# A hybrid encoder block: another order of the products, segment sums from running sums, and masked dt on ScalarE

## The reference

```
h = RMSNorm(x);  proj = h @ W_in        # columns: z | xBC | dt_f | dt_b | q | k | v | gate_a | gate_b
A: xBC = silu(centred depthwise conv of 5 taps);  xs, B, C = xBC   # 32 heads of 64, 8 groups, state 128
   per direction (forward, backward): dt = softplus(dt_raw + bias);  a = -exp(a_log) * dt
     chunks of 128 tokens, per head:
     decay[l,s] = exp(cumsum(a)[l] - cumsum(a)[s])   for s <= l, else 0
     y = (C B^T * decay * dt) @ xs  +  C @ state_in * exp(cumsum(a));  states pass between chunks
   y = y_f + y_b + d_skip * xs;  y = groupwise RMSNorm(y * silu(z)) * g;   branch_a = y @ W_ssm_up
B: q, k normed per head and rotated, softmax over all 256 tokens;  branch_b = y_attn @ W_attn_up
x = x + (sigmoid(gate_a) * branch_a + sigmoid(gate_b) * branch_b) @ W_out
x = x + relu(RMSNorm(x) @ W1)^2 @ W2;   out = RMSNorm(x)
```

## Time and profile before

| | |
|---|---|
| median of 3 runs | 1761.25 us |
| the profiled execution: its time | 1762.39 us |
| its span | 1760.6 us |
| mean granted TensorE clock | 0.981 of full speed |
| TensorE / ScalarE / VectorE / GpSimd busy | 1691.5 / 789.3 / 1071.3 / 210.3 us |
| DMA | 301.52 MB, mean 171 GB/s |

### The profile page before, as it was taken

The page is one execution under the profiler, slowest core; times in us unless marked ns, Lnnn a source line. Parts: engine busy times, 40 slices in busy tenths (PEclk is TensorE's granted clock), DMA queues, the critical chain, the costliest instruction groups (busy, mean ns, idle before and its releaser), DMA issues.

```text
span 1760.6 us, 21838 instructions
## 1 busy us (share of the span) xinstructions
PE 1691.5 (96%) x7734; PEld 1401.5 (80%) x7734; DVE 1071.3 (61%) x1190; ACT 789.3 (45%) x996; POOL 210.3 (12%) x178
## 2 busy tenths in 40 slices
PE   6888888899999999999999999999999999999997
PEld 5677677788888888888888888888888888888886
DVE  4989999966678855454545554455445544554453
ACT  4343333455455544444443445533553355335543
POOL 0445554400132200000000000000000000000000
PEclk8999989999999999999999999999999999999999
DMA  7344344456654456565655566566656665666663
GB/s 220 108 126 118 96 113 119 127 177 183 188 157 135 143 179 187 194 183 196 183 195 186 179 204 187 184 194 193 186 182 195 194 177 186 196 194 180 185 201 121
DMA packets 197222, 301.52 MB, mean 171 GB/s; under 512 B 14368, under 2 KB 70288, under 8 KB 197008
## 3 DMA queue, kind: packets, MB, share of 16 engines
q1 hardware_dynamic: 196960, 300.27, 56.4%
q10 hardware_dynamic: 176, 0.07, 0.0%
HBM read 298.20 MB, written 2.10 MB: 171 GB/s over the span
## 4 chain that ended last, share of the span: by engine, by line
issue 68%; PE 19%; DVE 9%; SPq 1%; DMA 1%; POOL 1%; ACT 0%; DVEq 0%; ACTq 0%; POOLq 0%
PE G L1216 5%; PE G L1217 5%; PE G L1218 5%; DVE acc L826 3%; DVE wlo L686 2%; PE S L1337 1%; DVE mw L876 1%; DVE acc L822 1%; DMA raw<-in_w_in 1%; DVE prob L973 0%; PE S L1224 0%; POOL q_rs L1097 0%; SPq L384 0%; PE S L1346 0%; DVE pT_lo L978 0%
## 5 line engine op out<-in xcount | busy, mean ns | idle before, releaser
L686 DVE TENSOR_TENSOR wlo<-raw,whi 128x1024 fp32r<-128x1024 f32 x560 | 698.7, 1253 | 514.3 <-ACT whi L425 514.2
L425 ACT ACTIVATE whi<-raw 128x1024 fp32r<-128x1024 f32 x560 | 593.8, 1060 | 883.8 <-PE G L1218 848.4
L1216 PE MATMUL G<-whi,a_hi 128*128 128x512 f32 x1344 | 538.2, 400 | 9.0 <-DVE wlo L686 9.0
L1217 PE MATMUL G<-wlo,a_hi 128*128 128x512 f32 x1344 | 529.8, 394 | 0.0
L1218 PE MATMUL G<-whi,a_lo 128*128 128x512 f32 x1344 | 529.2, 394 | 0.0
L1216 PEld LDWEIGHTS G<-whi,a_hi 128*128 128x128 f32 x1344 | 256.8, 191 | 61.7 <-DVE wlo L686 8.6
L1218 PEld LDWEIGHTS G<-whi,a_lo 128*128 128x128 f32 x1344 | 256.1, 191 | 55.4
L1217 PEld LDWEIGHTS G<-wlo,a_hi 128*128 128x128 f32 x1344 | 256.6, 191 | 51.1
L1216 PE MATMUL G<-whi,b_hi 128*128 128x512 f32 x640 | 250.5, 391 | 1.5 <-issue 1.5
L1218 PE MATMUL G<-whi,b_lo 128*128 128x512 f32 x640 | 249.2, 389 | 0.0
L1217 PE MATMUL G<-wlo,b_hi 128*128 128x512 f32 x640 | 249.0, 389 | 0.0
(11 more groups left out here) (188 smaller groups left out, 1347.2 us busy)
## 6 DMA issues: line engine op xcount, KB each, us to landing
raw<-in_w_in SPq DMA_DIRECT2D x136, 512.0 KB, 4.0
raw<-in_w_mlp_in SPq DMA_DIRECT2D x128, 512.0 KB, 3.8
raw<-in_w_mlp_out SPq DMA_DIRECT2D x128, 512.0 KB, 4.4
raw<-in_w_in SPq DMA_DIRECT2D x72, 256.0 KB, 2.8
raw<-in_w_in SPq DMA_DIRECT2D x144, 128.0 KB, 3.2
raw<-in_w_ssm_up SPq DMA_DIRECT2D x32, 512.0 KB, 4.4
raw<-in_w_attn_up SPq DMA_DIRECT2D x32, 512.0 KB, 4.5
raw<-in_w_out SPq DMA_DIRECT2D x32, 512.0 KB, 4.5
```

Source lines behind the costliest of these rows:

```text
L425: act.activation(whi[:, slot, 0:width], raw[:, slot, 0:width], ACT.Copy).then_inc(hi_made, 1)
L686: dve.tensor_tensor(wlo[:, slot, 0:width], raw[:, slot, 0:width], whi[:, slot, 0:width].bitcast(F32), ALU.subtract).then_inc(lo_made, 1)
L1216: pe.matmul(out_ap, hi[:, k, cols], w_hi, start=start, stop=False)
L1217: pe.matmul(out_ap, hi[:, k, cols], w_lo, start=False, stop=False)
```

## The change

1. **Order of the products.** The gates' eight products move from the merge into the scan stage: xbc 0, gate 0, xbc 1, gate 1 and so on. `conv(i)` is beside gate i, `scan(i-1)` and the gate's tanh beside xbc i. The tanh of all gates stays in a new tile `gates` of 8 blocks, whose first half is the place of `x_sb`; x is read again from HBM when the `out` products begin. The merge has only ssm_up and attn_up products, and its result goes to `a_hi`/`a_lo`.
2. **Segment sums.** Once, four small matmuls make the running sums of a for all 64 rows (32 heads, two directions), and `cum` and `neg_cum` hold them (high part in the first 64 partitions, low part in the others). Per group, `pick` selects rows: for each half (two heads) and direction TensorE does four matmuls of 256 columns, cum[l] - cum[s], into two banks; the smaller of the two directions is taken by VectorE after ScalarE has copied one (`f_made`, `seg_made`), then Exp.
3. **Masked dt** is 16 ScalarE copies of 128x128 with a scale operand per group; VectorE adds the two directions. GpSimd keeps `t2` only.
4. **The head.** The parameter DMAs are spread between pieces 5, 6, 7 and the next product's fifth; the dt product moves from piece 3 to piece 5; the dt chain's Exp and the steps behind it come later; the rope tables go to `tables` in window (1, 1).
5. The loop over the xbc windows runs 6 times over two windows (before: 2 times over two); the loop over the gates' windows is gone.

```diff
 def walk(eng, window):
     window(0, 0, "xbc", 0, [("rates", 0)])
-    window(0, 1, "xbc", 1, [("conv", 0), ("decays", 0)])
-    window(1, 0, "xbc", 2, [("conv", 1), ("scan", 0)])
-    window(1, 1, "xbc", 3, [("conv", 2), ("scan", 1)])
-    with eng.Fori(1, 3) as i:
-        window(i + 1, 0, "xbc", 2 * i + 2, [("conv", 2 * i + 1), ("scan", 2 * i)])
-        window(i + 1, 1, "xbc", 2 * i + 3, [("conv", 2 * i + 2), ("scan", 2 * i + 1)])
-    window(4, 0, "z", 0, [("conv", 7), ("scan", 6)])
...
+    window(0, 1, "gate", 0, [("conv", 0), ("decays", 0)])
+    window(1, 0, "xbc", 1, [("scan", 0), ("gate", 0)])
+    window(1, 1, "gate", 1, [("conv", 1), ("tables", 0)])
+    with eng.Fori(2, GROUPS) as i:
+        window(i, 0, "xbc", i, [("scan", i - 1), ("gate", i - 1)])
+        window(i, 1, "gate", i, [("conv", i)])
+    window(8, 0, "z", 0, [("scan", 7), ("gate", 7)])
...
-    with eng.Fori(0, 3) as j:
-        window(2 * j + 10, 0, "ssm_up", j, [("gate_b", j)])
...
+    window(13, 0, "ssm_up", 0, [("attend", 2), ("rope", 4)])
+    window(13, 1, "ssm_up", 1, [("attend", 3), ("gated_a", 0)])
...
+    window(15, 1, "attn_up", 1, [("merged", 0)])
...
@@ sync: window
-                if isinstance(r, int) and (r, par, p) == (0, 0, RING):
-                    parameters()
+                if isinstance(r, int) and (r, par, p) == (0, 0, 5):
+                    row_parameters()
+                if isinstance(r, int) and (r, par, p) == (0, 0, 6):
+                    rate_parameters(0, dt_bias_f, a_log_f)
+                    rate_parameters(1, dt_bias_b, a_log_b)
+                if isinstance(r, int) and (r, par, p) == (0, 0, 7):
+                    scan_parameters()
+                if isinstance(r, int) and (r, par, p) == (0, 1, 4):
+                    rope_parameters()
+                if kind == "out" and (idx, p) in ((0, 0), (1, 0)):
+                    sp.wait_ge(merge_v, 3 + idx)
+                    for c in range(3 * idx, 3 + idx):
+                        sp.dma_start(x_sb[:, c, :, :], x_k[:, :, c * N:(c + 1) * N]).then_inc(s_x[c], 16)
@@ scalar: decays
+            if p == 0:
+                act.wait_ge(dt_v, 4)
+                act.activation(u_dt[:, 2, :], u_dt[:, 1, :], ACT.Exp).then_inc(dt_e, 1)
...
+        def masked_dt(g, heads):
+            for h in heads:
+                for c in range(TB):
+                    for d in range(2):
+                        rate = dtv[:, c, d, ds(g * 4 + h, 1)]
+                        last = act.activation(mw[:, d, h, c, :], masks[:, 2 + d, :], ACT.Copy, scale=rate)
+            last.then_inc(mw_made, 1)
@@ scalar: conv
+            if p == 3:
...
+                act.activation(pick[:, :, :, :], sel[:, :, ds(g * 4, 4)].unsqueeze(3).to_broadcast([P, 2, 4, P]),
+                               ACT.Copy).then_inc(pick_made, 1)
+                masked_dt(g, (0,))
+            if p == 4:
+                masked_dt(g, (1, 2))
+            if p == 5:
+                masked_dt(g, (3,))
@@ scalar: scan
+            if p in (2, 4):
+                half = p // 2 - 1
+                act.wait_ge(fb_mm, 2 * g + (half + 1))
+                act.activation(ex[:, 2 * half:2 * half + 2, :].rearrange("p h l -> p (h l)"), S[:, 0, :], ACT.Copy
+                               ).then_inc(f_made, 1)
+            if p in (3, 5):
+                half = p // 2 - 1
+                act.wait_ge(seg_made, 2 * g + (half + 1))
+                part = ex[:, 2 * half:2 * half + 2, :].rearrange("p h l -> p (h l)")
+                act.activation(part, part, ACT.Exp).then_inc(ex_made, 1)
@@ vector: scan
+            if p == 0:
+                dve.wait_ge(mw_made, 3 * g + 3)
+                dve.tensor_tensor(w, w, mw[:, 1, :, :, :].rearrange("p h c l -> p h (c l)"), ALU.add
+                                  ).then_inc(scan_v, 1)
+            if p == 1:
+                dve.wait_ge(score_mm, g + 1)
...
+            if p in (2, 4):
+                half = p // 2 - 1
+                dve.wait_ge(f_made, 2 * g + (half + 1))
+                part = ex[:, 2 * half:2 * half + 2, :].rearrange("p h l -> p (h l)")
+                dve.tensor_tensor(part, part, S[:, 1, :], ALU.min).then_inc(seg_made, 1)
+            if p == 5:
+                dve.wait_ge(scan_v, step(2))
+                dve.wait_ge(ex_made, 2 * g + 2)
+                dve.tensor_tensor(w, w, ex[:, :, :], ALU.mult).then_inc(scan_v, 1)
@@ tensor: decays
+                for c in range(TB):
+                    for d in range(2):
+                        last = pe.matmul(S[:, 2, c * P:(c + 1) * P],
+                                         avx[:, c, d, :, :, :].rearrange("p a b h -> p (a b h)"), masks[:, 2 + d, :],
+                                         start=(d == 0), stop=(d == 1))
@@ tensor: scan
+            if p in (1, 3):
+                half = p // 2
+                if half:
+                    pe.wait_ge(seg_made, 2 * g + 1)
...
+                for d in range(2):
+                    for h in range(2):
+                        pe.matmul(S[:, d, h * T:(h + 1) * T], pick[:, d, 2 * half + h, :], cum[:, :],
+                                  start=(h == 0), stop=False)
+                    both = S[:, d, :].rearrange("p (h c l) -> p h c l", h=2, c=TB)
+                    for c in range(TB):
+                        last = pe.matmul(both[:, :, c, :], neg_cum[:, c * P:(c + 1) * P],
+                                         pick[:, d, 2 * half:2 * half + 2, :], start=False, stop=(c == TB - 1))
+                last.then_inc(fb_mm, 1)
...
+            if p == 6:
+                pe.wait_ge(scan_v, g * SCAN_V + 4)
+                for c in range(TB):
+                    for h in range(4):
...
+                last.then_inc(y_mm, 1)
```

More of the change, by code:

```diff
@@ L98, in walk @@
+    window(15, 0, "attn_up", 0, [("gated_a", 3)])
+    window(15, 1, "attn_up", 1, [("merged", 0)])
+    window(16, 0, "attn_up", 2, [("merged", 1)])
+    window(16, 1, "attn_up", 3, [("merged", 2)])
     window(17, 0, "out", 0, [("merged", 3)])
@@ L119, in piece_number, with landed_count @@
     return r * (2 * PIECES) + (PIECES * par + p)
[L122 to L128, removed]
+def landed_count(r, par, p, early):
+    if p >= PIECES:
+        r, par, p = (r + 1, 0, p - PIECES) if par else (r, 1, p - PIECES)
+    use = p // RING + 1
+    if early or (isinstance(r, int) and r <= GROUPS):
+        return r * 128 + (96 + 16 * use if par else 48 * use)
+    return r * 64 + (par * 32 + use * 16 + 64 * (GROUPS + 1))
 def previous(r, par):
@@ L172, in build @@
     raw = place("raw", [P, RING, 2 * N])
-    x_sb = place("x_sb", [P, TB, D])
+    gates = place("gates", [P, 2 * 4, TB, N])
+    x_sb = gates[:, 0:4, :, :]
     tmp_a = place("tmp_a", [P, TB, N])
@@ L654, in finish @@
                     final_squares(j, tb)
-        table = {f.__name__: f for f in (rates, decays, conv, scan, zgate, rope, values, attend, gate_a, gate_b,
-                                         merged, residual, hidden, finish)}
+        table = {f.__name__: f for f in (rates, decays, conv, scan, gate, zgate, rope, values, attend, merged,
+                                         residual, hidden, finish)}
         def window(r, par, kind, idx, sides):
@@ L662, in window @@
                 if not (isinstance(r, int) and 2 * r + par == U_END - 1 and q >= PIECES):
-                    threes = kind == "xbc" or (kind == "z" and idx == 0 and q < PIECES)
-                    split(piece_number(r, par, q), q % RING, 2 * N, landed_count(r, par, q, threes))
+                    early = kind in ("xbc", "gate")
+                    split(piece_number(r, par, q), q % RING, 2 * N, landed_count(r, par, q, early))
                 for name, at in sides:
@@ L997, in attend, with gated @@
                 low(1)
-        def gated(dst, pr, pp):
+        def gated(slot, pr, pp):
             dve.wait_ge(used, done(pr, pp))
@@ L1003, in gated @@
             for tb in range(TB):
-                last = dve.scalar_tensor_tensor(out=dst[:, tb, :], in0=dst[:, tb, :], scalar=1.0,
-                                                in1=product(pp, tb), op0=ALU.add, op1=ALU.mult)
+                part = gates[:, slot, tb, :]
+                last = dve.scalar_tensor_tensor(out=part, in0=part, scalar=1.0, in1=product(pp, tb),
+                                                op0=ALU.add, op1=ALU.mult)
             last.then_inc(taken[pp], 1)
@@ L1057, in finish @@
                     times_gain(j, tb)
-        table = {f.__name__: f for f in (rates, decays, conv, scan, zgate, rope, attend, gated_a, merged, residual,
-                                         hidden, add, finish)}
+        table = {f.__name__: f for f in (rates, decays, conv, scan, tables, zgate, rope, attend, gated_a, merged,
+                                         residual, hidden, add, finish)}
         def window(r, par, kind, idx, sides):
@@ L1122, in decays @@
[L1122 to L1130 removed]
         def scan(p, g, pr, pp):
             if p == 0:
+                if first(g):
```

(13 more changed lines are left out.)

364 lines of the change are left out of this document (147 added, 217 removed).

## The result

The changed kernel takes **1688.9 us** (median of 4 runs, 1688.56 to 1688.98); the kernel before, on the same chip, 1761.1 (1760.92 to 1761.45). The ratio is 0.9588, 95% interval 0.9577 to 0.9599: 72.2 us less. The forecast was 1695 with a range of 1688 to 1725.

The account below looks back on a forecast made before the run. TensorE, busy 1691.5 of 1760.6 us, was bound in the scan stage by waits for a late VectorE and the half clock after them. 71.7 us off and 5.7 on gave 1695, range 1688 to 1725.

Parts of the forecast that it names:

- Part 2: Scan stage: TensorE's seven stalls before the y matmuls go, minus 33.8 us, and half clock after them, minus 19.6.
- Part 1: Head, first two products: stalls and half clock go, minus 9.1 and 9.2 us; plus 1.7 and 0.8 for new delays.
- The late dt chain: Second product window: dt's Exp moves behind two ScalarE copies, so weight pieces 3 and 5 come late, plus 1.7 us.
- Part 3: TensorE's side work per scan group: 16 matmuls of 256 columns replace eight of 512, plus 0.7 us.
- The interruptions: Main product interrupted at five places per group instead of seven, 0.1 us each: up to 1.6 us less.
- Part 4: Loops: scan's has five back edges instead of one, the gates' loop goes; 0 to 5 us, taken as plus 2.5.
- At nothing: Masked ScalarE copies, reload of x, moved gated products and merge priced at zero; rope tables 0 to 1 us.
- The first rival: Scan and convolution windows: ScalarE or a hand-over late by a few us per pair; 1705 to 1730 us, chance 0.22.
- The wait changes place: Scan groups: last product still misses y as much as now, 61 of 66 us lost; about 1752, chance 0.06.
- GpSimd was not the cause: Convolution windows: taps take 1.2 us whoever else runs, so the kernel gets slower; about 1790 us, chance 0.05.

Follow-up runs that it names:

- version 1: Kernel before, old order, GpSimd's masked rates and masked dt made for the first group only and reused: 1708.8 us, ratio 0.970.
- version 2: Kernel before with only the new order of products (gates between xbc products, scan and convolution in separate windows), GpSimd keeping its masked work: 1718.3 us, ratio 0.9755.
- version 3: Changed kernel with 12 unused GpSimd multiplications of 128x512 per group beside the convolution's taps: 1763.5 us, ratio 1.0011.
- version 5: Kernel before, old order, GpSimd masks for first group only, plus new ScalarE and VectorE work without the running-sum matmuls: 1708.2 us, ratio 0.9697.
- version 4: Changed kernel with all 15 small parameter DMAs back in one block ahead of the fifth weight piece: 1700.8 us, ratio 0.9652.
- the eighth: The changed kernel run again unaltered, on one chip with two versions that move operands in SBUF: 1688.7 us, ratio 0.9584.
- version 6: Changed kernel with the `out` products' stationary operand put back on `m_hi` and `m_lo` instead of `a_hi` and `a_lo`: 1690.6 us, ratio 0.9594.

## Why the prediction was right, and 6 us too high

The direction, the mechanism and most terms held.

- **Part 2, the scan's stalls (33.8 + 19.6).** Right: all seven stalls and the half clock behind them are gone. The cause, GpSimd beside VectorE, is shown from three sides (versions 1, 2 and 3). What the prediction had wrong is what the order is for. It gave the hand-overs room by the new windows and counted "4.5 to 5.6 missing" without them; versions 1 and 5 have no stall in the scan in the old order. The two cures overlap wholly. By the starts of the products, seven windows with convolution and scan took 259.1 us before, and the seven gates that now stand between them 7 x 21.76 alone: 411.4. Reckoned in the same way version 1 (GpSimd quiet) takes 357.4, version 5 357.2, version 2 (the order alone) 357.3, and the changed kernel 357.3. Each cure alone brings all the 54 us of this stage; with GpSimd quiet, the order adds nothing there. Over the whole kernel version 1 is worth 53 us and all of the change 72. Version 2 is worth only 43, for it loses some 10 at the MLP's loop.
- **Part 1, the head (9.1 and 9.2 off, 1.7 and 0.8 on).** Right. The first product is 9.1 us shorter, as forecast (39.34 to 30.23), and version 4 brings a stall back by the order of the DMAs alone. The second product is 6.95 us shorter (33.86 to 26.91) where 9.2 less 1.7 and 0.8 makes 6.7. Its stall of 6.9 us stays in version 1 as long as GpSimd works beside those taps (9.73 us for eight) and is gone in the changed kernel, where eight take 3.26. The late dt chain, priced at 1.7, is 0.79 (0.48 and 0.31). That these two products come within 0.2 of the forecast is in part luck: the 0.9 gained there are nearly offset, for TensorE's side work in the second product grew by 1.5 us instead of 0.8 (it is busy 26.12 us both times, and before 1.5 of that were lost to half clock); the first group's four score matmuls, some 0.4 us, stand in it now. Version 1's profile ends 19.2 us behind the changed kernel's: 16.3 by the start of the third product, 0.1 in the stage of the scan, 2.8 behind it.
- **Part 3, the side work.** Eight 256-column matmuls take 0.94 us, 0.1175 each, against the 0.119 taken: plus 0.5 instead of plus 0.7. The interruptions, kept for the low end, seem to have come: the seven pairs of windows of Part 2 gained 54.1 us (411.4 to 357.3), where the prediction's terms make 50.3; 2.5 of the 3.8 are loop edges, 0.2 are these 256-column matmuls, and 1.1 are left, against 1.4 for two places less in each of seven groups. No run shows the interruptions by themselves. By the formula in the Trainium skill, "TensorE: Matmul & The Clock Gate", back-to-back issue gap, which that page gives for a matmul by itself, one would estimate 109 ns for them; the trace has 117.5, so the row was the better guide.
- **Part 4, the loops (plus 2.5).** Wrong by 3.3: the scan's five back edges cost TensorE nothing, as the zero end of the range had it (y follows y after 51.04 us inside the loop as before it), and the MLP's two cost 0.7 instead of 1.5. Those two vary from one execution or version to the next, from nothing (the eighth, which is the same kernel) to 3.3 and 3.7 (the second), so no part of the change need be the cause of this difference.
- **At nothing.** The masked copies step by 0.29 us inside a run of eight, (2.44 - 0.39) / 7. That agrees with the estimate of 0.29 from the Trainium skill's figures ("ScalarE: Activation LUTs", what a table load costs) and is near the low end of the prediction's; a copy is 0.387 us long, so neighbours overlap by 0.09, not by the 0.03 that the prediction put into that low end. The first rival, a late hand-over, stayed out. The slack of `cs` is 1.7 to 1.8 us, as forecast, and 0.5 where the tables stand in the same window: they took 1.2 to 1.3 of it, not all. The reload of x delays nothing.
- **Not in the prediction:** `out` reads `a_hi` and `a_lo`, minus 2.4 by the steps; version 6 gives 1.7 back.

The account, by the starts of the products: 16.0 us were gained up to the start of the third product (forecast 15.8), 54.1 in the seven pairs of windows (forecast 50.3), and 3.3 behind them (forecast minus 0.1, the eighth group's side work), 73.4 in all against 66.0. Of the 7.4 that the forecast missed, 0.2 lie in the head, 3.8 in the stage of the scan (2.5 of them loop edges), and 3.4 behind it, where the place of the operand gives 2.4 and the MLP's edges 0.8. The rivals fell as their conditions did. "The wait changes place" needed 7 us more in the chain (its own terms, 61 of 66 us gone, give 1756 and not 1752). "GpSimd was not the cause" is refuted by versions 1 and 3.

## What to carry to other kernels

When an engine's instructions take twice as long in some stretches, look at who runs beside them before counting its work. The cure may be to take that neighbour's work away or to move it beside something else; try each alone, for their gains need not add: here either brought all of it. And spread small DMAs behind the weight pieces that are asked for first.

## What the runs showed of the hardware that was not expected

- The price of GpSimd beside VectorE: a tap 1.26 us instead of 0.47, with nothing between, so 856 to 866 ns instead of 476 in the mean of all taps; a 128x512 product of two SBUF tensors 1222 to 1487 ns instead of 682 in mean. The first tap (L822), which reads one tensor, is slower too: in the kernel before 0.40 us with GpSimd quiet and 1.13 beside it (medians of 10 and of 22). The 128x512 product with one input from PSUM (L860) took 684 ns in mean before, though GpSimd ran beside 11 of its 16, and in version 1 alike.
- The place of a stationary operand in SBUF costs up to 6.4 ns per 512-column matmul, 2.8%. In all that was measured, products are slow whose low tile starts at 193728 or above, in all three passes, and, if they start at a multiple of 128 bytes, quick where both tiles end by 180864. Whether the high tile has a bound of its own, and where it is, stays open; so does why a start 64 bytes past a multiple of 128 costs 10.3 us over 2112 x 3 matmuls, but spares the pass with `wlo`.
- A wait at a back edge of the MLP's loop is 0 to 3.7 us in one kernel's variants, and at the two long ones (3.3 and 3.7 us, version 2) there is a half-clock stretch too.
